# Row-wise division of probabilities on VectorE, and the channel norm's mean subtraction and inverse root on GpSimd, in a diffusion backbone step

## The reference

```python
def layernorm(x, g, b):
    xf = x.astype(jnp.float32)
    mu = jnp.mean(xf, axis=-1, keepdims=True)
    var = jnp.mean(jnp.square(xf - mu), axis=-1, keepdims=True)
    return ((xf - mu) * lax.rsqrt(var + EPS) * g + b).astype(x.dtype)

    def attend_block(qs):
        qn, qr = qs
        s = jnp.einsum("bqhd,bkhd->bhqk", qn, k_nope) + jnp.einsum("bqhr,bkr->bhqk", qr, k_rope)
        p = jax.nn.softmax(s.astype(jnp.float32) * ATTN_SCALE, axis=-1).astype(v.dtype)
        return jnp.einsum("bhqk,bkhd->bqhd", p, v)
...
    z = a * jax.nn.sigmoid(gate)
    z = lax.conv_general_dilated(z, conv_w[:, None, :], (1,), [(CONV_PAD, CONV_PAD)],
                                 dimension_numbers=("NWC", "WIO", "NWC"),
                                 feature_group_count=C_CONV) + conv_b
    return jax.nn.silu(layernorm(z, ln_g, ln_b))
```

## Time and profile before

| | us |
|---|---|
| runs, median (lowest to highest of 3) | 1307.95 (1307.94 to 1309.65) |
| the profiled execution, its time | 1308.96 |
| its span in the trace | 1307.1 |
| PE busy | 1218.6 (93%) |
| DVE busy | 639.5 (49%) |
| ACT busy | 404.5 (31%) |
| POOL busy | 175.0 (13%) |

### The profile page before, as it was taken

How to read it: one execution, slowest core, us unless ns; L and a number is a source line. 1 busy time by engine, 2 the same in 40 slices (tenths; PEclk the granted TensorE clock), 3 DMA queues, 4 the chain that set the end, 5 groups by cost and what they waited for, 6 DMA issues and landing times.

```text
span 1307.1 us, 19051 instructions
## 1 busy us (share of the span) xinstructions
PE 1218.6 (93%) x7036; PEld 810.0 (62%) x7037; DVE 639.5 (49%) x1347; ACT 404.5 (31%) x770; POOL 175.0 (13%) x173
## 2 busy tenths in 40 slices
PE   4899999899999899999998999998989989999992
PEld 1545555455544688888877555555664458888881
DVE  1265978243426633433332579784552663333333
ACT  2100213344443313322323002135564331332233
POOL 4000101230200011222220000021210001122220
PEclk9899999999999989999999999999999998999996
DMA  9883430756481539989997000103007154999966
GB/s 369 257 338 134 73 122 0 290 174 215 163 290 65 212 123 332 287 229 339 304 249 183 1 1 5 57 1 129 1 1 274 65 199 151 328 336 331 329 176 191
DMA packets 139388, 239.34 MB, mean 183 GB/s; under 512 B 23394, under 2 KB 106304, under 8 KB 133184
## 3 DMA queue, kind: packets, MB, share of 16 engines
q1 hardware_dynamic: 120736, 186.70, 42.0%
q0 software_dynamic: 11712, 28.73, 9.9%
q10 hardware_dynamic: 6880, 23.08, 4.5%
HBM read 216.10 MB, written 31.82 MB: 190 GB/s over the span
## 4 chain that ended last, share of the span: by engine, by line
PE 85%; DMA 5%; DVE 4%; ACT 3%; issue 2%; ACTq 0%; SPq 0%; DVEq 0%; POOLq 0%
PE ps L1345 51%; PE ps L1632 11%; PE ps L1516 4%; PE ps L1538 4%; PE ps L1371 3%; PE ps L1549 3%; DMA region_h<-in_w_ada 2%; PE ps L1694 2%; DMA x_rows<-region_proj,row_out 2%; DVE region_h L880 1%; DMA x<-x_rows 1%; PE ps L1527 1%; PE ps L1517 1%; PE ps L1351 1%; ACT region_weights L749 1%
## 5 line engine op out<-in xcount | busy, mean ns | idle before, releaser
L987 DVE SCALAR_TENSOR_TENSOR region_bc<-region_conv,vecs,region_bc 128x655 f32<-128x655 f32 x240 | 202.0, 904 | 0.9
L1345 PE MATMUL ps<-region_h,region_weights 128*128 128x128 f32 (+1 forms) x512 | 141.0, 437 | 1.5 <-ACT region_h L682 1.5
L1345 PEld LDWEIGHTS ps<-region_conv,region_weights 128*128 128x128 f32 x1088 | 124.0, 192 | 9.3 <-issue 7.2
L1345 PEld LDWEIGHTS ps<-region_conv,region_oq 128*128 128x128 f32 x1088 | 124.2, 192 | 8.1 <-issue 8.1
L1345 PE MATMUL ps<-region_conv,region_weights 128*128 128x128 f32 x1088 | 124.4, 275 | 1.8 <-DVE region_conv L1310 1.8
L1345 PE MATMUL ps<-region_conv,region_oq 128*128 128x128 f32 x1088 | 124.2, 275 | 0.0
L1345 PEld LDWEIGHTS ps<-region_h,region_weights 128*128 128x128 f32 x512 | 78.3, 192 | 66.3 <-issue 64.5
L880 DVE TENSOR_TENSOR region_proj<-ps,region_proj 128x128 f32<-128x128 f32 (+1 forms) x89 | 27.8, 312 | 183.6 <-ACT region_proj L853 161.9
L1068 DVE TENSOR_REDUCE att_stat<-ps 128x1 f32<-128x640 f32 (+1 forms) x68 | 55.5, 816 | 114.2 <-PE ps L1517 109.3
L853 ACT ACTIVATE region_proj<-ps 128x128 f32<-128x128 f32 x68 | 18.9, 277 | 251.8 <-PE ps L1345 243.4
L1345 PE MATMUL ps<-region_oq 128*128 128x512 f32 (+2 forms) x304 | 94.2, 471 | 2.7 <-issue 2.1
(11 more groups left out here) (238 smaller groups left out, 1679.6 us busy)
## 6 DMA issues: line engine op xcount, KB each, us to landing
region_h<-in_w_ada SPq DMA_DIRECT2D x26, 1024.0 KB, 5.0
region_oq<-in_w_ada SPq DMA_DIRECT2D x20, 1024.0 KB, 9.3
region_weights<-in_w_gate SPq DMA_DIRECT2D x16, 1024.0 KB
region_weights<-in_w_up SPq DMA_DIRECT2D x16, 1024.0 KB
region_weights<-in_w_down SPq DMA_DIRECT2D x16, 1024.0 KB
region_oq<-in_w_gate SPq DMA_DIRECT2D x16, 1024.0 KB
region_oq<-in_w_up SPq DMA_DIRECT2D x16, 1024.0 KB
region_oq<-in_w_down SPq DMA_DIRECT2D x16, 1024.0 KB
```

Source lines behind the costliest of these rows:

```text
L987: ins = nc.vector.scalar_tensor_tensor(acc[:, ct, :], zpad[:, ct, j:j + CONV_OUT], w, acc[:, ct, :], ALU.mult, ALU.add)
L1345: ins = nc.tensor.matmul(out, lhs(k), rhs(k), start=(k == 0), stop=(k == n - 1))
```

## The change

Five things are changed, all in the attention stage.

1. The exponentials aren't spread and multiplied in at the output any more. DVE takes the reciprocal of each unit's row sums and multiplies the 640 probabilities of a row by it in place (`scale(i)`, called divide(i) in the prediction; in context units by a broadcast over four heads). `spread` goes, with its waits, its columns in `probT` and the context copy; output(g) becomes a plain copy.
2. PE's order in a unit becomes scores(i+2), then turn(i), which waits for divide(i). ACT's becomes exp(i+1), then copy(i).
3. The scale of the scores is put into the rotary table that the queries are multiplied by, and the maximum is written negated, so the small product on DVE goes. The scaled sum and the epsilon are put in where DVE copies the norm's sums out of PSUM.
4. ACT runs an exponential of one column before the first unit, and no root inside attention.
5. POOL subtracts the mean itself, four subtractions beside its four squares, and takes the sum to the power -0.5 in one instruction of 128x655, in place of ACT's root and DVE's four reciprocals.

```diff
@@ constants
+    tab *= SCALE
@@ POOL, inside attention
+                pool.wait_ge(ln_mean, 2 * (l + 1))
                 for k in range(CC):
-                    pool.wait_ge(ln_centred, CC * l + k + 1)
+                    step(nc.gpsimd.tensor_tensor(acc[:, k, :], acc[:, k, :], ln_rstd, ALU.subtract))
                     step(nc.gpsimd.tensor_tensor(zsq[:, k, :], acc[:, k, :], acc[:, k, :], ALU.mult))
...
-                pool.wait_ge(ln_rstd_ready, l + 1)
+                pool.wait_ge(ln_var, 2 * (l + 1))
+                step(nc.gpsimd.tensor_tensor(ln_rstd, ln_rstd, minus_half[:, 0:1].broadcast_to([P, CONV_OUT]), ALU.pow))
                 for k in range(CC):
                     nc.gpsimd.tensor_tensor(acc[:, k, :], acc[:, k, :], ln_rstd, ALU.mult).then_inc(ln_done, 1)
@@ ACT
+                nc.scalar.activation(stat[:, 63:64], eps_t[:, 0:1], ACT.Exp)
                 exponential(0)
                 for i in range(UNITS):
-                    turned(i)
-                    if i == LN_ROOT:
-                        act.wait_ge(ln_var, 2 * (l + 1))
-                        nc.scalar.activation(ln_rstd, ln_rstd, ACT.Sqrt, scale=1.0 / CONV_C, bias=eps_t[:, 0:1]).then_inc(ln_sqrt, 1)
                     if i + 1 < UNITS:
                         exponential(i + 1)
-
-                act.wait_ge(ctx_spread, l + 1)
-                act.wait_ge(att_out, GROUPED * l + LAT_GROUPS)
-                nc.scalar.activation(probT[2][:, 0:4 * P], ps[:, 5], ACT.Copy).then_inc(ctx_spread_ready, 1)
+                    turned(i)
@@ DVE
-                    step(nc.vector.reduce_max(s_max[:, cols], src, AXIS_X))
-                    nc.vector.tensor_scalar(s_neg[:, cols], s_max[:, cols], -SCALE, None, ALU.mult).then_inc(att_max, 1)
+                    nc.vector.reduce_max(s_neg[:, cols], src, AXIS_X, negate=True).then_inc(att_max, 1)
+
+                def scale(i):
+
+                    h, t, cols = unit_parts(i)
+                    dve.wait_ge(att_exp, UNITS * l + i + 1)
+                    step(nc.vector.reciprocal(s_inv[:, cols], s_sum[:, cols]))
+                    if t < LAT:
+                        ins = nc.vector.tensor_scalar(prob[:, i % 2], prob[:, i % 2], s_inv[:, cols], None, ALU.mult)
+                    else:
+                        p4 = prob[:, i % 2, 0:4 * P].rearrange("p (h n) -> p h n", h=4)
+                        ins = tt(p4, p4, s_inv[:, cols].unsqueeze(2).broadcast_to([P, 4, P]), ALU.mult)
+                    ins.then_inc(prob_scaled, 1)
...
-                        tt(attT[:, pr, t * P:(t + 1) * P], ps[:, 6, 0:P], spread, ALU.mult).then_inc(att_out_empty, 1)
+                        nc.vector.tensor_copy(attT[:, pr, t * P:(t + 1) * P], ps[:, 6, 0:P]).then_inc(att_out_empty, 1)
...
-                        nc.vector.scalar_tensor_tensor(acc[:, k, :], ln_rstd, -1.0 / CONV_C, acc[:, k, :], ALU.mult, ALU.add).then_inc(ln_centred, 1)
...
-                        step(nc.vector.reciprocal(ln_rstd[:, a:b], ln_rstd[:, a:b]))
...
                 for i in range(UNITS):
-                    if i % 2 == 1 and i >= 3:
-                        inverse_sums((i - 3) // 2)
+                    if i == 2:
+                        scale(0)
+                    if i >= 2:
+                        scale(i - 1)
                     maximum(i)
@@ PE
                 for i in range(UNITS):
-                    turn_prob(i)
                     if i + 2 < UNITS:
                         score(i + 2)
+                    turn_prob(i)
```

75 lines of the change are left out of this document (23 added, 52 removed).

## The result

The changed kernel takes **1496.87 us** (median of 4 runs, 1495.77 to 1498.83) where the kernel before takes 1308.12 (4 runs): 1.145 times as long, interval 1.143 to 1.146. The prediction said 1332 with 1376 as its upper end. The sign and the stall came as forecast, the size did not. The profiled execution took 1495.77 us, its span is 1493.9.

The account below looks back on a forecast made before the run. TensorE, busy 92% of attention, was taken as the bound, with ScalarE equally late in layer 1's ordinary pairs. 1308.96 - 13.0 without the power + 37 for the powers, less 1.0, gave 1332 us; range 1294 to 1376 (8 in 10).

Parts of the forecast that it names:

- The sign: Whole kernel: slower after the change, chance 0.64, against 0.30 for faster and 0.06 for within 0.2%.
- the stall: VectorE's multiply beside GpSimd's power stands still, TensorE runs dry: 17.4 us in layer 1, 16.4 in layer 0.
- the size of the power: GpSimd's 128x655 power, one a layer, after unit 21's second variance copy: 18 us each.
- a long power: Rival: GpSimd's power takes over 30 us; 50 us give 1396, 65 give 1426; chance 0.16.
- The sum's form 1295.9 + 2P: Whole kernel's time in us for a blocking power of P us in each layer; the sign turns at P = 6.0.
- The third rival: GpSimd's power doesn't stop VectorE, up to 28 us of it hidden: 1295 us; chance 0.30 together with a short power.
- the price of the spreads: TensorE's products spreading inverse sums after even units' turns, 16 a layer: 0.56 us a pair, 9.0 us in layer 0.
- The ring wins: 5.2 a pair: Layer 1: serial maximum, exp, reciprocal, multiply take 2.6 us a unit against TensorE's 2.48; pairs 5.2 instead of 5.51.
- The start: Attention's first units: Exp table loaded earlier, scaling of the maximum gone; -1.4 us in layer 1, -0.7 in layer 0.
- The root: ScalarE's root inside attention goes with its two table loads: -3.2 us in layer 1, -3.9 in layer 0.
- Collisions: VectorE's new multiplies meet GpSimd instructions in attention, about 8 in layer 1: +6.0 us there, +2.5 in layer 0.
- The end: Attention's end: context sums' spread goes, a reciprocal and 512-column multiply precede the last turn; about +0.2 us a layer.

Follow-up runs that it names:

- the run with two pieces: The changed kernel with each power split into two instructions of 328 and 327 columns, one after the other: 1439.5 us.
- the run with the old order: The changed kernel with the power on 6 columns and TensorE's transposes again ahead of the scores two units on: 1296.5 us.

## Why the prediction was wrong

The step that failed is **the size of the power**. "Two such long steps at 5.6 times GpSimd's 2.23 ns a column" made 18 us from VectorE's reciprocal, and the power takes 104.8: 160 ns a column, 72 times the 2.23 of a product there. Even the upper bound of 65 us fell. It took 99 ns for a one-column instruction as the most that a column can cost, and that was a fill with a constant: a power of one column takes 668 ns, of which some 0.5 us are its start. Neither another engine's iterated operation nor another operation of GpSimd bounded it. What came true is the rival "a long power", with a power longer than the 65 us that it reached to. The sum's form 1295.9 + 2P gives 1505.5 with the measured P, 8.6 us over the time: 5.0 of them are the parts beside the power (18.0 gained instead of 13.0), and 3.6 the stalls, which cost 207.0 where the form has 2P + 1.0 = 210.6.

**The stall was right** for this kernel: one multiply as long as the power, TensorE idle, the clock low after it (0.55 in the 4.5 us behind it in layer 0 and 0.50 in layer 1, where the next step is 4.66 instead of 2.63). It was right in part by luck: the prediction had a stall as long as the power whatever its width, while one of 552 columns, a sixth narrower, holds the multiply for 0.37 us. The rule of the Trainium skill that was weighed (SBUF — State Buffer, "Who interferes with whom": a tensor_scalar in the two-port mode takes the pair that GpSimd holds for its whole instruction) agrees with the 104.34 us of the multiply. The Trainium skill (VectorE: DVE Perf Modes, "Mode 2×_2P") wants a single source for that mode, in SBUF like the result, with an outermost dimension that is even, or odd and equal in both. That agrees with what stood (4 and 640 columns) and with what read PSUM and passed; for the one column that passed its words don't decide. The first of these rules does not foresee that beside powers of up to 552 columns the same multiply waits 0.37 us at most and not for the whole instruction, and there the measurement decides. The third rival, a power that doesn't stop VectorE, is nearly true up to that width. At its measured length it would not have given 1295, though: the run with two pieces gave 1439.5, since the work behind the power comes late.

The terms beside it, from the steps without a power:

- Layer 0 gains 6.6 us (forecast, with collisions, 9.6), layer 1 11.4 (forecast 3.4), together 18.0 instead of 13.0.
- **Spreads and pairs.** 0.56 us a pair was right as the price of the spreads, as the run with the old order shows; the new order gives 0.09 of it back. "The ring wins: 5.2 a pair" was wrong. Its parts were right, but neighbours on VectorE overlap by 0.08 (the next maximum starts 0.47 after the multiply's start, not 0.55), the hand-overs are shorter by 0.1, and the whole takes 2.44, under TensorE's 2.52. Layer 1's pairs gain 0.47 instead of 0.31.
- **The start** was forecast at -1.4 in layer 1. It gave -3.8 (10.48 to 6.69 us for four steps). With the old order it is 10.0, so 3.3 of it come from the order with scores first and only 0.5 from the table load and the scaling. The prediction had no term for that. In layer 0 it was -0.6, as forecast (-0.7), since the weight piece's wait takes it back.
- **The root**: layer 1's step of 5.93 would be 2.63, -3.3 (forecast -3.2). In layer 0 units 24 to 31 gain 5.3 us, and the forecast has 3.9 for the root and some 1.7 for the pairs. Right.
- **Collisions** were forecast at 6.0 in layer 1 and cost 2.05 (four steps of 2.7 to 3.4). Eight multiplies meet GpSimd, as forecast: six ahead of the power, 0.5 to 0.8 us longer, and two behind it that cost no step. The prediction let every one reach TensorE, and about half of what the six lost was slack. In layer 0 they cost 2.0 (forecast 2.5), most of it in one step (4.25 instead of 2.41, from unit 13's scores to unit 14's), ahead of which six small instructions on 8 columns meet GpSimd, two of them 1.24 and 1.05 us instead of 0.17.
- **The end** came out -0.2 in layer 1, and +1.8 in layer 0 without the power, where the granted clock was 0.63 in the last 6.5 us instead of 1.00 (both forecast at +0.2).

## What to carry to other kernels

Before an operation is moved to an engine, look for a row of that operation on that engine. Without one, a bound from another operation or engine can be many times off, so ask how few elements need the operation: here 6 columns did the work of 655, and made a loss of 189 us a gain of 13, or 16 with GpSimd's other instructions cut in two. An instruction that stops another engine should be short: a collision costs what is left of the other's instruction, so that cutting it in pieces brings the wait under the slack. And a long instruction on a queue has two prices, what it stops and what stands behind it; when the first is taken away the second shows (here 131 us of 189 were left).

## What the runs showed of the hardware

- GpSimd's power (fp32, both operands in SBUF) costs about 0.5 us and 159 ns a column: 0.67 us for 1 column, 1.21 and 1.41 for 5, 23.1 for 143, 52.7 for 328, 82.0 for 512, 104.8 for 655. The number of partitions was varied once only (15 rows with one column: 0.54).
- Beside it a VectorE multiply of 128x640 from SBUF to SBUF stands still to the power's end if that has 584 columns or more. With 512, 520 and 552 columns it waits only until 0.84 to 0.91 us after the power's start, and then runs in its ordinary 0.55 us. Beside a power of 655 columns a scaling of 128x4 stood as well (one row), while scalings of 128x1, reciprocals of up to 4 columns and what reads PSUM passed.
- GpSimd's plain two-input instructions hold up the same multiply at 655 columns (1.02 to 1.38 us) and at 328 (0.70 to 0.98).
- A DMA that GpSimd issues waits in its program's order behind a long instruction: VectorE waited 79.8 us for the bias load behind a power and four products.
